# A decoder trunk's main matmuls stream their columns in another order: two halves woven together

## The reference

```python
for i in range(DEPTH):                      # DEPTH = 2
    hp = rmsnorm(xp, g_mix_pre[i]); hs = rmsnorm(xs, g_mix_pre[i])
    if i % 2 == 0:
        op, ... = even_prompt(hp, w_in_even[j], w_out_even[j], conv_w[j], attn_sinks[j])
    else:
        op, ... = cmlp_prompt(hp, w_in_cmlp[j], w_out_cmlp[j], ...)
    xp = xp + rmsnorm(op, g_mix_post[i])
    xp = xp + rmsnorm(ffn(rmsnorm(xp, g_ffn_pre[i]), w_ffn_up[i], w_ffn_down[i]), g_ffn_post[i])
    # the same for the samples, xs

def ffn(h, w_up, w_down):
    a = jax.nn.relu(h @ w_up)
    return (a * a) @ w_down
```

## Time and profile before

| | |
|---|---|
| median of 3 runs | 2230.07 us (2228.09 to 2232.19) |
| the profiled execution, whole | 2228.98 us |
| its span, first to last instruction | 2227.3 us |
| TensorE matmuls busy | 2176.4 us, 98% |
| TensorE weight loads busy | 2154.9 us, 97% |
| VectorE busy | 1249.9 us, 56% |
| ScalarE busy | 995.6 us, 45% |
| DMA | 386.72 MB, mean 174 GB/s |
| granted TensorE clock, mean | 0.990 |

### The profile page before, as it was taken

One profiled execution on the slowest core, in us unless ns is written; L12 is line 12 of the kernel. 1 busy time (PEld: TensorE's weight loads), 2 busy tenths in 40 slices (PEclk: granted clock), 3 DMA queues, 4 the chain that ended last, 5 costly groups with the idle time before them and its releaser, 6 DMA issues.

```text
span 2227.3 us, 43497 instructions
## 1 busy us (share of the span) xinstructions
PE 2176.4 (98%) x17771; PEld 2154.9 (97%) x17771; DVE 1249.9 (56%) x1318; ACT 995.6 (45%) x1243; POOL 236.9 (11%) x178
## 2 busy tenths in 40 slices
PE   7999998999999999999989999989999999999999
PEld 7999998999999999999979999979999999999998
DVE  7556756654554455455576675575445545545543
ACT  5545444443443344344454564444334434434443
POOL 3001213000000000011251201220000000001112
PEclk9999998999999999999999999989999999999999
DMA  6854453655655655565535455545555555555551
GB/s 218 232 171 136 155 183 113 189 177 181 187 174 186 215 181 186 176 185 172 186 114 188 155 170 181 178 127 176 188 175 183 183 177 187 174 184 183 176 181 65
DMA packets 380630, 386.72 MB, mean 174 GB/s; under 512 B 6804, under 2 KB 378316, under 8 KB 380430
## 3 DMA queue, kind: packets, MB, share of 16 engines
q1 hardware_dynamic: 374530, 380.02, 54.4%
q10 hardware_dynamic: 6036, 5.80, 0.8%
HBM read 380.10 MB, written 5.71 MB: 173 GB/s over the span
## 4 chain that ended last, share of the span: by engine, by line
PE 92%; DVE 6%; ACT 1%; DMA 0%; issue 0%; DVEq 0%; SPq 0%; ACTq 0%
PE ps L1353 30%; PE ps L1355 30%; PE ps L1354 30%; DVE hlo L979 2%; DVE wlo L952 1%; DVE y L1001 1%; ACT whi L586 0%; PE ps L1635 0%; DMA region<-in_x_prompt_dram 0%; PE ps L1704 0%; PE ps L1548 0%; PE ps L1534 0%; PE ps L1467 0%; DVE region L1336 0%; DVE y L1006 0%; DVE x L1007 0%
## 5 line engine op out<-in xcount | busy, mean ns | idle before, releaser
L952 DVE TENSOR_TENSOR wlo<-raw,whi 128x1024 fp32r<-128x1024 f32 x712 | 895.2, 1261 | 805.0 <-ACT whi L586 804.6
L586 ACT ACTIVATE whi<-raw 128x1024 fp32r<-128x1024 f32 x712 | 752.3, 1059 | 1066.4 <-PE ps L1355 1061.3
L1353 PE MATMUL ps<-hhi,whi 128*128 128x264 f32 x3136 | 902.6, 288 | 33.4 <-DVE hlo L979 33.1
L1354 PE MATMUL ps<-hlo,whi 128*128 128x264 f32 x3136 | 895.4, 286 | 0.0
L1355 PE MATMUL ps<-hhi,wlo 128*128 128x264 f32 x3136 | 895.3, 285 | 0.0
L1353 PE MATMUL ps<-ahi,whi 128*128 128x264 f32 x2560 | 727.0, 284 | 0.0
L1355 PE MATMUL ps<-ahi,wlo 128*128 128x264 f32 x2560 | 726.8, 284 | 0.0
L1354 PE MATMUL ps<-alo,whi 128*128 128x264 f32 x2560 | 726.6, 284 | 0.0
L1353 PEld LDWEIGHTS ps<-hhi,whi 128*128 128x128 f32 x3136 | 595.5, 190 | 43.5 <-issue 30.1
L1355 PEld LDWEIGHTS ps<-hhi,wlo 128*128 128x128 f32 x3136 | 595.4, 190 | 0.0
L1354 PEld LDWEIGHTS ps<-hlo,whi 128*128 128x128 f32 x3136 | 595.1, 190 | 0.1
(11 more groups left out here) (218 smaller groups left out, 763.6 us busy)
## 6 DMA issues: line engine op xcount, KB each, us to landing
raw<-in_w_ffn_up_dram SPq DMA_DIRECT2D x128, 1024.0 KB, 5.3
raw<-in_w_ffn_down_dram SPq DMA_DIRECT2D x128, 1024.0 KB, 5.5
raw<-in_w_in_even_dram SPq DMA_DIRECT2D x36, 1024.0 KB, 5.1
raw<-in_w_in_cmlp_dram SPq DMA_DIRECT2D x32, 1024.0 KB, 5.3
raw<-in_w_out_even_dram SPq DMA_DIRECT2D x16, 1024.0 KB, 5.5
raw<-in_w_out_cmlp_dram SPq DMA_DIRECT2D x16, 1024.0 KB, 5.6
region<-in_x_prompt_dram SPq DMA_DIRECT2D x4, 512.0 KB, 9.1
out_y_prompt_dram<-region SPq DMA_DIRECT2D x8, 256.0 KB
```

The source lines that it names most:

```text
L586: act.activation(whi[:, QK * q:QK * q + QK, :], raw[:, 2 * par + q // 2, k, :], ACT.Copy).then_inc(w_hi_ready, 1)
L952: dve.tensor_tensor(wlo[:, QK * q:QK * q + QK, :], raw[:, 2 * par + q // 2, k, :], whi[:, QK * q:QK * q + QK, :].bitcast(F32), ALU.subtrac ...
L1353: pe.matmul(out, whi[:, k, cols], hi[:, k, ::-1], start=(k == 0), stop=False)
L1354: pe.matmul(out, whi[:, k, cols], lo[:, k, ::-1], start=False, stop=False)
```

## The change

Each main matmul walks its moving operand and its output in a new order. `woven` views the 264 columns as two halves of 132 (`h`), each of 33 groups of four (`c`), and goes over the groups outermost, the halves next, and the four words innermost, all three backwards. The columns come in the order 263, 262, 261, 260, then 131, 130, 129, 128, then 259 and so on. Weights, waits and all else stay.

```diff
+            def woven(ap):
+                return ap.rearrange("p (h i c) -> p i h c", h=2, c=4)[:, ::-1, ::-1, ::-1]
...
-                        out = ps[:, 2 * par + j, 0:T][:, ::-1]
-                        pe.matmul(out, whi[:, k, cols], hi[:, k, ::-1], start=(k == 0), stop=False)
-                        pe.matmul(out, whi[:, k, cols], lo[:, k, ::-1], start=False, stop=False)
-                        mm = pe.matmul(out, wlo[:, k, cols], hi[:, k, ::-1], start=False, stop=(k == CH - 1))
+                        out = woven(ps[:, 2 * par + j, 0:T])
+                        pe.matmul(out, whi[:, k, cols], woven(hi[:, k, :]), start=(k == 0), stop=False)
+                        pe.matmul(out, whi[:, k, cols], woven(lo[:, k, :]), start=False, stop=False)
+                        mm = pe.matmul(out, wlo[:, k, cols], woven(hi[:, k, :]), start=False, stop=(k == CH - 1))
```

## The result

The change made the kernel 8.2% slower: 2413.73 us (median of 4) against 2229.23, ratio 1.0824, 95% interval 1.0805 to 1.0843. The forecast was 2230 with a range up to 2315.

What follows compares the result with a forecast made beforehand. TensorE's row of 17,088 main matmuls was taken to bound the kernel. The only term, 17,088 x d with d = 0, left the median of 2,230.07, so 2230 us was forecast, with an 8-in-10 range of 2160 to 2315.

Steps and rivals of the forecast that it cites:

- What bounds the kernel: Whole kernel: it is as long as its row of 17,088 main matmuls on TensorE, busy 98%, 120.8 ns each.
- d: Change of the start-to-start distance of main matmuls, the only term; taken as 0, bounded from -9 to +65 ns.
- the last 10 ns: In every main matmul at full clock, some 10 ns of 120 are not array time and don't follow the clock.
- I take d = 0: Main matmuls: breaks cost nothing, judged from line 1500, whose broken access showed 0.1 ns for a break.
- That reservation: On the nearest rows: they are plain fp32 at half the words per ns, they are short, and ends are modelled.
- The second reason: Main matmuls: operand and weight tiles shift mutual position with every k, yet the distance stays 0.12 us, so position seems not to matter.
- The contention step: Main matmuls beside VectorE's `wlo` subtraction: eleven starts at 123.6 ns each laid to contention, 14 us in all.
- Rivals B and C: Main matmuls' contention with VectorE: more of it, about 2290 us, chance 0.19; or less, 2216 us, chance 0.19.
- Write to PSUM, other engines, DMA: Around the matmuls: broken output costs nothing; ScalarE needs 1.06, VectorE 1.26 us per 2.9 us quarter; DMA delivers 185 GB/s.
- Rival A: Address step between runs, in read or PSUM write: every break costs, +17 ns (2520 us) or 2690 us; chance 0.14.
- Rival D: Main matmuls: part or all of the 10 ns is owed to the order; 2145 us or 2076 us, chance 0.08.

Runs made afterwards that it cites:

- operand_one_word: Kernel before, but the moving operand is the first word of each tile 264 times over: 2100.16 us, ratio 0.9422.
- near_two: Changed kernel's order replaced by runs of two words, the two that change places lying in the same 16-byte stretch: 2229.48 us, ratio 1.0000 to the kernel before.
- write_woven: Changed kernel with only the output written in woven order, the operand read backwards in one run: 2230.10 us, ratio 1.0002 to the kernel before.
- near_swap: Changed kernel's runs of four words, but the two runs that change places are neighbours within each eight words: 2234.25 us, ratio 1.0020 to the kernel before.
- mixed: Kernel before, with operand and output taking other orders in tiles 2, 3, 10 and 11: 2222.57 us, ratio 0.9967.
- ladder: Two kernels: one-word weight loads, output backwards, operand's paired runs of four a different distance apart per tile; 2284.41 and 2245.87 us, 1.0248 and 1.0076 to the kernel before.
- runs_of_two: Changed kernel with runs of two words in place of four, so each 16-byte stretch is visited twice: 3093.59 us, ratio 1.3872 to the kernel before.

## Why the prediction was wrong

**What bounds the kernel** was right: the time went with the distance of main matmuls, d x 17,088 gave the loss to 6 us, no wait of TensorE moved, and the half clock kept its 0.22 us. That the last 10 ns are not array time and sit in something that doesn't follow the clock was right too, and `operand_one_word` says what: some 8 of them are the read of the moving operand going from one 16-byte stretch to the next.

**The step that failed** is "I take d = 0, as the broken line 1500 is the row nearest in form". Line 1500 is nearest in form, and form is free: `near_two` has 131 breaks and costs nothing. The term d was put at 0 and measured 11.1 ns (131.9 - 120.8), 190 us. It is set by which stretches the moving read visits one after another at the full rate of delivery. Line 1500 reads at most half the words per ns, and two stretches in all, so it could not show it. That reservation stood in the text, its last line named this very step as the one to fail, and it was given no weight in the time. (The plain matmul of line 1370 is a still weaker witness than it was taken for: 222 ns is the distance between its records, and the trace lists two for each matmul.)

**The second reason given was a misreading.** "The stream seems not to care for where its words lie" rested on a timeline written to 0.01 us. To the ns, the same trace shows 124 and 123 at tiles 2 and 3 and a repeat after 8 tiles, 256 bytes: the sign, available beforehand, that position matters.

**The contention step** put the eleven slow distances to VectorE's subtraction because it ran beside them. With weight loads that read one word the subtraction ran on and the distances were even. Rivals B and C were built on that, and their common mechanism falls. The contention that is there, between TensorE's two reads, is 1.2 of the 11.1 ns.

**Write to PSUM, other engines, DMA**: nothing, as forecast; `write_woven` shows it for the write.

**Rival A** had the right sign. Its place, "the address step between runs", was wrong, its price (17 to 27 ns) too high: the measured 11 ns are 0.17 per break if shared out so, but `near_swap` shows that a break as such costs next to nothing. Its argument that the stream already runs at a limit that the array does not set was the one to weigh more.

**Rival D** put the 10 ns down to the order. Most of them do belong to the read, but no full walk of the operand that was tried gives them back: forwards is slower, and `mixed` gives 0.4 ns.

**What stays open.** The memory's layout behind the ladder's numbers isn't settled. That reads about 8, 16, 24 and 32 stretches apart disturb one another is measured; why the window is wide around 8 and 24 and narrow around 16 and 32 is not explained, and the reading by direct hops and later visits is not tested. Nor is it known what the second visit alone costs in `runs_of_two`. Nor is the reason why forwards is 1.2% slower than backwards, beyond the sign that it too depends on the tile.

## What to carry to other kernels

Where float32r matmuls with their weight loads follow one another at full clock, the order in which the moving operand's 16-byte stretches are read is part of the cost; walk through them once, one after another. If two places must alternate, measure their distance: the costly ones here lay at and near multiples of 128 bytes, and turning the order inside the pair took nine tenths of the cost away at the same distance. A row that has the same form of access pattern but asks less of the memory says nothing on the price at full rate; take the distance from start to start to the ns and sort it by tile before holding that position doesn't matter. When two rows run side by side, take one away before you call it contention.

## What the runs showed of the hardware

- The moving operand's delivery holds a float32r matmul of 264 columns at 120 ns at full clock; with the read kept in one 16-byte stretch the median is 112 (mean 113.2). The array's share is 110, an estimate from the 220.0 ns at the 1.2 GHz level.
- A matmul whose operand is read in 132 runs of two words takes 120.9 ns when each stretch is visited once, and 172.5 when each is visited twice with a far hop between. The Trainium skill, "SBUF — State Buffer", Specifications, gives 16-byte lines with a penalty for each change to a new one and full bandwidth from two hits per line. The first half agrees with these runs. Two hits, taken as enough, do not: `runs_of_two` has two at each visit and takes 172.5 ns, the changed kernel has four and takes 131.9.
- Whether a woven read costs anything depends on the distance of its two places, 118 to 120 ns for 28, 30 or 31 stretches and 127 to 133 for 32 and 33, and on which of the two is read first: at 33 stretches 132 ns one way and 122 the other.
- The operand's read and the weight load's read disturb one another at some mutual positions, by 2 to 3 ns on the mean of tiles 2, 3, 10 and 11 of the kernel before, with a period of 256 bytes, and hardly at the others.
- The output to PSUM may be written in broken runs without cost: runs of four words that alternate between two halves (`write_woven`, ratio 1.0002), and runs of two words that change places with their neighbour (`near_two`, 1.0000).
